# One product of the normed rows moved into each attention, in single steps between its units

## The reference

```python
gates = jax.nn.sigmoid(gate_logits.reshape(b, s, N_BRANCHES, d) + b_gate)
merged = gates[:, :, 0] * (o_a @ w_proj_a) + gates[:, :, 1] * (o_b @ w_proj_b)
x = x + (merged @ w_out)
```

## Time and profile before

| | |
|---|---|
| runs | 3157.65 us median of 3 (3156.02 to 3158.03) |
| profiled execution | span of the core 3155.9 us; the page gives no other time of it |
| TensorE busy | 2956.2 us, 94% |
| VectorE, ScalarE, GpSimd busy | 39%, 24%, 4% |
| mean granted clock of TensorE | 0.971 |

### The profile page before, as it was taken

One profiled execution on the slowest core, in us unless ns is written; L12 is line 12 of the kernel. 1 busy time (PEld: TensorE's weight loads), 2 busy tenths in 40 slices (PEclk: granted clock), 3 DMA queues, 4 the chain that ended last, 5 costly groups with the idle time before them and its releaser, 6 DMA issues.

```text
span 3155.9 us, 43167 instructions
## 1 busy us (share of the span) xinstructions
PE 2956.2 (94%) x15320; PEld 2056.7 (65%) x15321; DVE 1215.3 (39%) x2572; ACT 751.5 (24%) x1483; POOL 116.9 (4%) x132
## 2 busy tenths in 40 slices
PE   8989899998999999899899879898999999999999
PEld 7874667655585556386357668586776596776774
DVE  6770773242212221211212156535333355444432
ACT  3221751111212121211211023514111225232111
POOL 0000100000000000000000000011000000110000
PEclk9999999988999999999999989899999999999999
DMA  4222012257999999999999452021321220112221
GB/s 171 81 67 79 3 41 80 74 204 298 395 364 365 419 413 390 416 379 382 408 415 391 149 201 95 1 87 49 108 84 54 100 95 27 61 61 87 81 80 67
DMA packets 137804, 577.60 MB, mean 183 GB/s; under 512 B 15981, under 2 KB 21485, under 8 KB 87504
## 3 DMA queue, kind: packets, MB, share of 16 engines
q1 hardware_dynamic: 128176, 558.87, 46.6%
q0 software_dynamic: 9504, 17.07, 1.4%
HBM read 572.47 MB, written 20.97 MB: 188 GB/s over the span
## 4 chain that ended last, share of the span: by engine, by line
PE 85%; DVE 5%; DMA 5%; ACT 2%; issue 2%; DVEq 1%; SPq 0%; POOLq 0%; ACTq 0%
PE banks L395 31%; PE banks L1521 13%; PE banks L1497 9%; PE banks L332 8%; PE banks L1027 7%; PE banks L1471 6%; DMA arena<-in_w_experts 5%; PE banks L800 3%; PE banks L823 2%; PE banks L811 2%; PE banks L271 1%; DVE arena L873 1%; DVE arena L885 1%; PE banks L1451 1%; PE banks L1926 1%
## 5 line engine op out<-in xcount | busy, mean ns | idle before, releaser
L395 PE MATMUL banks<-arena 128*128 128x256 f32 (+2 forms) x4704 | 1015.3, 377 | 21.6 <-ACT arena L432 7.4
L395 PEld LDWEIGHTS banks<-arena 128*128 128x128 f32 x4704 | 883.8, 192 | 142.0 <-issue 21.5
L1521 PEld LDWEIGHTS banks<-arena 128*128 128x128 f32 x3584 | 403.8, 193 | 14.5 <-issue 14.5
L1521 PE MATMUL banks<-arena 128*128 128x128 f32 x3584 | 405.5, 277 | 4.7 <-issue 4.7
L1497 PE MATMUL banks<-arena 128*64 128x512 f32 (+1 forms) x1024 | 322.6, 593 | 0.0
L1471 PE MATMUL banks<-arena 128*64 128x512 f32 x1152 | 268.3, 616 | 24.9 <-DMA arena<-in_w_experts 22.3
L1599 DVE TENSOR_TENSOR arena<-banks,arena 128x512 f32<-128x512 f32 x64 | 44.3, 692 | 614.1 <-PE banks L1521 351.9
L432 ACT ACTIVATE arena<-banks 128x512 f32<-128x512 f32 (+2 forms) x168 | 98.7, 588 | 690.9 <-PE banks L395 690.9
L448 DVE TENSOR_TENSOR arena<-banks,arena 128x512 f32<-128x512 f32 (+2 forms) x126 | 85.7, 680 | 436.2 <-PE banks L395 434.7
L332 PE MATMUL banks<-arena 128*128 128x512 f32 x576 | 250.0, 593 | 0.0
L1497 PEld LDWEIGHTS banks<-arena 128*64 128x64 f32 (+1 forms) x1024 | 123.5, 159 | 176.1 <-issue 176.0
(11 more groups left out here) (210 smaller groups left out, 2041.0 us busy)
## 6 DMA issues: line engine op xcount, KB each, us to landing
arena<-in_w_experts SPq DMA_DIRECT2D x384, 1024.0 KB, 19.3
arena<-in_w_in SPq DMA_DIRECT2D x84, 1024.0 KB, 5.0
arena<-in_w_out SPq DMA_DIRECT2D x12, 1024.0 KB, 5.0
arena<-in_w_branch SPq DMA_DIRECT2D x24, 512.0 KB, 4.7
arena<-expert_rows SPq DMA_DIRECT2D x4, 2048.0 KB, 14.4
arena<-in_w_in SPq DMA_DIRECT2D x4, 832.0 KB, 4.6
arena<-in_gate_b SPq DMA_DIRECT2D x2, 1536.0 KB, 6.5
arena<-in_x SPq DMA_DIRECT2D x4, 512.0 KB, 5.3
```

What stands on the lines that cost most here:

```text
L395: last = PE.matmul(PS[:, bank, t * width:(t + 1) * width], one[:, t * P:(t + 1) * P], other, start=(first and t == 0 and kk == 0), stop=(t ...
L1521: last = PE.matmul(PS[:, q, f * P:(f + 1) * P], gate_up(q, k)[:, f * P:(f + 1) * P], xT[:, k], start=(f == 0 and k == 0), stop=(f == 3 and ...
```

## The change

In each attention 32 plain calls (4 row tiles by 8 steps of the contraction, 512 columns each) are issued by TensorE between the parts of its units. They make one product in bank 7; VectorE takes each finished tile out. The values of all pairs use bank 6.

- dilated and grouped: the logits of gate 0, first 512 columns, tiles 0, 2, 1 in units 4 to 15 of dilated and tile 3 in units 0 to 7 of grouped. In a layer's chunk attention the same, four units a tile.
- latent attention: `z` of the chunk branch, transposed, in units 2 to 15. Its weights are loaded behind the attention's fence into the place of raised queries and another free one.
- The merges begin with `branch` of branch 0; their first `Quarters` product is that of branch 1, and its weights are the ones issued ahead.
- The chunk heads have three products in place of four; sigmoid and multiplication of `z` run beside the first. They also load the gate's weights and bias, into places of their own.

The diff, cut:

```diff
@@ attention
+            def steps_of(u):
+                for t, (first, last) in enumerate(fill["units"] if fill else ()):
+                    if first <= u <= last:
+                        n, at = last - first + 1, u - first
+                        return list(range(8 * t + at * 8 // n, 8 * t + (at + 1) * 8 // n))
+                return []
+            def value_bank(p):
+                return 6 if fill else 6 + p % 2
+                def filling(steps):
+                    for n in steps:
+                        t, kk = n // 8, n % 8
+                        if n == 0:
+                            fill["ready"](pe, c)
+                        if kk == 0:
+                            pe.wait_ge(SEM[fill["out_sem"]], up(fill["out_count"](c) + t))
+                        last = PE.matmul(PS[:, 7], fill["still"](fill["tiles"][t], kk), fill["moving"](fill["tiles"][t], kk),
+                                         start=(kk == 0), stop=(kk == 7))
+                        if kk == 7:
+                            last.then_inc(SEM["fill_mm"], 1)
                 def values(u):
                     if i == 0:
-                        pe.wait_ge(SEM["o_done"], up(c.of("pairs") + p - 1))
+                        pe.wait_ge(SEM["o_done"], up(c.of("pairs") + p - (0 if fill else 1)))
                     if u + 2 < units:
                         scores(u + 2)
+                    steps = steps_of(u)
+                    filling(steps[:len(steps) // 2])
                     turn(u)
+                    filling(steps[len(steps) // 2:])
                     if u:
                         values(u - 1)
+                def filled(u):
+                    for n in steps_of(u):
+                        if n % 8 == 7:
+                            if n == 7:
+                                fill["ready_out"](dve, c)
+                            dve.wait_ge(SEM["fill_mm"], up(c.of("filled") + n // 8 + 1))
+                            fill["out"](fill["tiles"][n // 8], PS[:, 7]).then_inc(SEM[fill["out_sem"]], 1)
                 for u in range(units):
+                    if u:
+                        filled(u - 1)
                     if u + 2 < units:
                         top(u + 2)
                     if u + 1 < units:
                         norm(u + 1)
-                    if u % TT == 1 and u > TT:
+                    if u % TT == (0 if fill else 1) and u >= TT:
                         finish(u // TT - 1)
@@ attention_first
+            def next_gates(sp, c):
+                sp.wait_ge(SEM["fill_mm"], up(c.of("filled") + 1))
+                merge_1.lead(sp, c)
...
@@ merge_stage
             def lead(sp, c0):
-                dense_sp(sp, c0, 0, gate_weights(c0, 0, 0))
+                dense_sp(sp, c0, 0, gate_weights(c0, 0, 1))
...
-                        if n + b:
-                            dense_sp(sp, c, b, gate_weights(c0, n, b), quartered=b, done=-n * nbr)
+                        if n or b > 1:
+                            dense_sp(sp, c, b, gate_weights(c0, n, b), quartered=of_gates(n, b), done=-n * nbr)
                         sp.wait_ge(SEM["mm"], up(4 * (c.of("M") + b)))
...
-                        Q(c).pe(pe, c, 2 * b, b, hooks=hooks)
-                        branch(pe, c, b)
+                        if n or b:
+                            Q(c).pe(pe, c, b + of_gates(n, b), of_gates(n, b), hooks=hooks)
+                        branch(pe, c, n, b)
@@ latent_stages
+            def z_sp(sp, c):
+                sp_after(sp, c)
+                src = w2(c).rearrange("(k p) n -> p k n", p=P)[:, :, bass.ds(4000, 512)]
+                sp.dma_start(v2(QM, 6, 512), src[:, 0:6]).then_inc(SEM["fill_w"], 16)
+                sp.dma_start(v2(QST + 512, 2, 512), src[:, 6:8]).then_inc(SEM["fill_w"], 16)
+            z_fill = {"tiles": (0, 1, 2, 3), "units": ((2, 5), (6, 9), (10, 12), (13, 15)), ...
+                      "out": lambda t, ps: V.tensor_copy(v(YC + 512 * t, 512), ps)}
@@ chunk_stages
-            lead, sp0, pe_, act0, dve0 = fast_hT(0, [(c0s + 1536, 512), (c0s, 512), (c0s + 512, 512), (c0s + 1024, 512)],
-                                                        across=(0, 1, 2))
+            lead, sp0, pe_, act0, dve0 = fast_hT(0, [(c0s, 512), (c0s + 512, 512), (c0s + 1024, 512)], across=(0, 1))
...
+            gate_fill = {"tiles": (0, 1, 2, 3), "units": ((0, 3), (4, 7), (8, 11), (12, 15)), ...
+                         "out": lambda t, ps: V.tensor_tensor(v(early_gate(t), 512), ps, v(GATE_B, 512), ALU.add)}
```

More of the change, by code:

```diff
@@ L778, in attention @@
             first_group = [sum(groups_of[x % TT] for x in range(u)) for u in range(units + 1)]
-            KC = {"u": units, "g": first_group[units], "pairs": 4, "biased": 4 if a.get("sp") else 0}
+            fill = a.get("fill")
+            KC = {"u": units, "g": first_group[units], "pairs": 4, "biased": 4 if a.get("biased") else 0}
+            if fill:
+                KC["filled"] = len(fill["tiles"])
+                KC |= fill["counts"]
+            def steps_of(u):
[6 more added lines that the diff above has]
+                return 6 if fill else 6 + p % 2
             def prob(u, s):
@@ L1047, in sig, with part @@
                             act.wait_ge(SEM["sig_in"], up(c.of("sig") + 4 * b + tt + 1))
-                            g = v(GS + 512 * tt, 512)
+                            g = v(GS + 512 * tt if n or b else early(tt), 512)
                             AC.activation(g, g, ACT.Sigmoid).then_inc(SEM["sig_out"], 1)
+                        def part(i):
+                            Q(c).act(act, c, b + of_gates(n, b), of_gates(n, b), i)
+                        if not n + b:
+                            for tt in range(TT):
+                                sig(tt)
+                            continue
                         def back(tt):
@@ L1981, in finish, with z_weights @@
                 return V.tensor_tensor(o, ps, o, ALU.mult)
-            return latents, raised, turned, attention({"turn": (PTS, PTS + 1024), "scale": MLA_SCALE, "W": W_, "finish": finish,
+            def z_weights(kk):
+                return v(QM + 512 * kk, 512) if kk < 6 else v(QST + 512 * (kk - 5), 512)
+            def z_sp(sp, c):
+                sp_after(sp, c)
+                src = w2(c).rearrange("(k p) n -> p k n", p=P)[:, :, bass.ds(4000, 512)]
+                sp.dma_start(v2(QM, 6, 512), src[:, 0:6]).then_inc(SEM["fill_w"], 16)
+                sp.dma_start(v2(QST + 512, 2, 512), src[:, 6:8]).then_inc(SEM["fill_w"], 16)
+            z_fill = {"tiles": (0, 1, 2, 3), "units": ((2, 5), (6, 9), (10, 12), (13, 15)), "counts": {"fw": 2, "z_out": 4},
+                      "ready": lambda pe, c: pe.wait_ge(SEM["fill_w"], 16 * c.of("fw") + 32),
+                      "still": lambda t, kk: z_weights(kk)[:, t * P:(t + 1) * P], "moving": lambda t, kk: hT[:, kk],
+                      "out_sem": "z_out", "out_count": lambda c: c.of("z_out"), "ready_out": lambda dve, c: None,
+                      "out": lambda t, ps: V.tensor_copy(v(YC + 512 * t, 512), ps)}
+            return latents, raised, turned, attention({"fill": z_fill, "sp": z_sp, "turn": (PTS, PTS + 1024), "scale": MLA_SCALE, "W": W_, "finish": finish,
                 "scores": lambda p, s, i: [(v(MQT + s * 512 + p * 1024 + i * P, P, 96),
@@ L2056, in finish, with chunk_sp @@
                 return V.tensor_tensor(o, ps, o, ALU.mult)
-            return heads, attention({"turn": (LB + 6144, LB + 7168), "scale": ATT_SCALE, "W": W_, "finish": finish, "pool": biases, "sp": rows_of,
+            def chunk_sp(sp, c):
+                merge_2.lead(sp, c)
+                rows_of(sp, c)
+            gate_fill = {"tiles": (0, 1, 2, 3), "units": ((0, 3), (4, 7), (8, 11), (12, 15)), "counts": {"fw": 2},
+                         "ready": lambda pe, c: pe.wait_ge(SEM["fill_w"], 16 * c.of("fw") + 32),
+                         "still": lambda t, kk: hT[:, kk, t * P:(t + 1) * P], "moving": lambda t, kk: v(GATE_W + 512 * kk, 512),
+                         "out_sem": "sig_in", "out_count": lambda c: c.of("sig"), "ready_out": lambda dve, c: None,
+                         "out": lambda t, ps: V.tensor_tensor(v(early_gate(t), 512), ps, v(GATE_B, 512), ALU.add)}
+            return heads, attention({"fill": gate_fill, "biased": True, "turn": (LB + 13162, LB + 14186), "scale": ATT_SCALE, "W": W_, "finish": finish, "pool": biases, "sp": chunk_sp,
                 "scores": lambda p, s, i: [(v(CQK + p * 512 + i * P, P, E, E * s),
@@ L2121, in build @@
         heads_1 = project_first()
-        dilated, grouped = attention_first()
         merge_1, turn_last_1, mT = merge_stage(
@@ L2158, in _ @@
             heads_1.sp(sp, c)
-            merge_1.lead(sp, c)
+            dense_sp(sp, c, 0, lambda h: rows(w_in, 8, h, 5376, 512))
             dilated.sp(sp, c)
```

114 lines of the change are left out of this document (70 added, 44 removed).

## The result

The changed kernel takes 3161.11 us (median of 20 runs, 3156.51 to 3168.27); the kernel before, on the same chip, takes 3156.32 (20 runs, 3149.74 to 3161.78). The ratio is 1.0016, 95% interval 1.0009 to 1.0022: 5.0 us slower, between 2.8 and 6.9. That lies inside the 0.2% that the prediction called no change for most of its interval. It forecast 3161.5, or 3.9 more.

A forecast was written before the change was run, and what follows sets the result against it. TensorE was taken as the bound, holding 85% of the chain of waits. 137.4 - 121.7 - 28.1 - 15.0 + 24.4 + 6.9 = +3.9 us; 3161.5 us predicted, from a median of 3157.65, range over the cases 3149 to 3177.

The forecast's parts named there:

- Removed, 121.7: Merges and head projections: five products by quarters go, 24.47 + 2 x 24.41 + 2 x 24.2 = 121.7 us.
- Added, 137.4: Attentions: five plain products of 32 steps, 0.86 us a step, add 5 x 64 x 0.429 = 137.4 us.
- Hidden waits: Attentions: steps cover 28.1 us of TensorE's waits (bounds 20 and 32): grouped 0.8, latents 13.0, chunks 14.3.
- The dilated 0.31: Dilated unit: TensorE's 0.31 us wait inside the transposes gets no step, so it stays.
- four copies out of the bank ... fit: Latent attentions: VectorE, busy 12.05 of 16.5 us, has room for four copies of some 0.7 us each.
- Clock won back, 15.0: Latent and chunk attentions: without pauses the clock recovers, 6.8 in latents, 7.4 and 0.8 in chunks, 15.0 us (bounds 0, 20.7).
- Rival A: Attentions: the lower clock is not won back, price 15.0 us; +18.9 on the time before, 3176.5; chance 0.22.
- The new wait, 24.4: Merges: branch 0's product waits for weights issued behind fence and bias broadcast, 7.8 + 2 x 8.3 = 24.4 us.
- Rival B: Merges: weights pass or run beside the bias broadcast, waits 4.5 each; 11 less, low clock 2 less: -9, 3148.5; chance 0.12.
- The low clock after it, 6.9: Merges: after TensorE's pause of 8 us the clock is low, losing 2.3 at each, 6.9 us (bounds 0 and 10).
- Rival C: Attentions: 18 handovers of the single bank for values stall 0.7 us each; +12.6 on the forecast, 3174; chance 0.07.
- Rival D: Attentions: VectorE and ScalarE freed, clock wholly back also in starts (20.7), grouped hides 2.2; -3.2, 3154.5; chance 0.12.

The follow-up runs named there:

- experiment 7: Changed kernel with the dilated attention's step ahead of the transposes put inside them, before the third group: 3152.55 us, ratio 0.9991 to the kernel before.
- experiment 11: Changed kernel with the layers' first branch weights loaded during the chunk attention and the dilated step inside the transposes: 3133.59 us, ratio 0.9927 to the kernel before.
- experiment 10: Changed kernel with the layers' first branch weights loaded during the chunk attention into places of their own: 3139.11 us, ratio 0.9943 to the kernel before.
- experiment 1: Kernel before with only the z projection filled into the two latent attentions: 3145.03 us against 3154.33, ratio 0.9964.
- Experiment 6: Changed kernel with the eight z steps of a tile all in one unit of the latent attentions: 3178.13 us, ratio 1.0065 to the kernel before.
- experiment 2: Kernel before with only the first block's gate 0 filled into dilated and grouped, its merge starting with the branch product: 3172.93 us, ratio 1.0064.
- experiment 4: Changed kernel with the first branch's weights issued ahead of the gate bias broadcast in each merge: 3151.50 us, ratio 0.9990 to the kernel before.
- experiment 5: Changed kernel with eight unused calls ahead of each merge's first branch product: 3154.70 us, ratio 0.9997 to the kernel before.
- experiment 9: Changed kernel with the first block as in the kernel before, the layers' z and gate fills kept: 3147.56 us against 3155.82, ratio 0.9974.

## Why the prediction was right, step by step

**Removed, 121.7.** Right: the quarter products' line fell by 560 records, the head stages by 24.2 each.

**Added, 137.4.** Nearly: 0.88 in the dilated units and 0.86 in the grouped ones where 0.858 was taken. The charge that I named and left out was 0.05 for a step standing alone; dilated shows about half of it, grouped none.

**Hidden waits.** The dilated 0.31 stayed as said, and experiments 7 and 11 show that it was on the path. Grouped absorbed 1.6 us, but hid nothing: its waits for normalised probabilities are 3.5 us before and 3.7 after. What it won is clock, on which the prediction counted nothing there. Behind the same first wait the transposes ran at the lower clock before (granted 0.50) and at the full one after (1.00):

```profile
PE banks L811 <- DVE arena L885: 3.5, 4, 1.7
...
PE banks L827 <- DVE arena L916: 3.7, 3, 1.7
...
406.98 1.97 PE L811 MATMUL banks<-arena 128*128 128x128 f32 x8 [1.67 <-DVE arena L885]
...
431.34 1.10 PE L827 MATMUL banks<-arena 128*128 128x128 f32 x8 [1.67 <-DVE arena L916]
```

That the clock did not fall here in this profile is luck: in experiments 7, 10 and 11 the filled grouped attention has 3.4 us at the lower clock in its first units and takes 62.7 to 62.9 in place of 61.3.

In the chunk attentions 16.5 became 1.8, so 14.7 where 14.3 was said, and the wait that stays at the start is 0.9 (predicted 1.1):

```profile
2167.45 0.44 PE L827 MATMUL banks<-arena 128*128 128x128 f32 x2 [0.92 <-DVE arena L916]
```

In the latents 13.0 was too much. At unit 0 of the first latent TensorE waits 1.33 us, before the steps begin (unit 2). In the kernel before there was no such wait, because the first scores ran at the lower clock (granted 0.50, 5.46 us where they now take 3.24). And twice in each a step waits 0.33 us for the copy of the tile before out of bank 7, a wait that the prediction had no term for ("four copies out of the bank ... fit"). The two on TensorE's timeline:

```profile
2021.59 0.44 PE L827 MATMUL banks<-arena 128*128 128x128 f32 x2 [1.33 <-DVE arena L916]
...
2043.31 1.13 PE L838 MATMUL banks<-arena 128*128 128x512 f32 x2 [0.33 <-DVE arena L2073]
```

13.0 less 1.7, 0.3 and twice 0.6 leaves 9.8 in this pair. Over all profiles TensorE stands 7.0 us on the mean in an unfilled latent and 1.6 in a filled one, 10.9 in two. That is the mis-sized term: the latents with their heads gained 11.1 by the table and 11.3 by experiment 1, where 13.2 was forecast. In the chunk attentions the same count gives 9.3 and 1.5, so 15.7 in two.

**Clock won back, 15.0.** The lower level is a granted 0.50 (2022 to 2027 us of the kernel before). The 15.0 were worked out from rows 6: 8.71 us at 0.61 lose 3.4, taken once in each latent attention, and the four stretches of the chunk attentions lose 2.6, 2.7, 3.9 and 4.7, 6.5 of it at the starts. The expectation was right: all four attentions run at 1.00 past their starts. In the chunk attentions 25.0 of the 55.0 us were absorbed, 15.7 of it waits, so about 9.3 is clock (8.2 forecast). In the latents 17.7 were absorbed, 10.9 of it waits, so about 6.8 (6.8 forecast). The granted clock says the same: an unfilled chunk attention spends 6.8 to 17.1 us at the lower level, a filled one none in twenty; a latent 3.4 to 16.5 unfilled (11.2 on the mean) and 0 to 10.2 filled (4.3), all of it in the first 12 us. The exact 6.8 is luck. The prediction counted one stretch in each latent, where the first latent before has three, and did not say that the one at the start would mostly stay. Experiment 6 ties the clock to the waits: spacing the same steps so that the waits return brings the low clock back. Rival A had this failing; it is out. The tie is not strict, though. In experiment 2 the first latent attention (from 2013.21) is that of before and waits, and its clock does not fall before 2060; it took 52.31, the least of the six. Its waits up to 2056 and the stretch:

```profile
PE banks L827 <- DVE arena L916: 5.4, 4, 1.4
...
2000.00:2056.00 56.00, 47.17 (x316) 30.45 (x314) 34.89 (x142) 33.08 (x90) 0.00 (x0) 1.00 0.00 1
```

**The new wait, 24.4.** Right: with the fence's own 1.25 and 1.83 taken off, 6.8 + 2 x 8.4 = 23.6. Just under half of it (11.0) comes from the order of the two issues, which experiment 4 turns round. It is Rival B's mechanism, as something that one can do and not as something that the change did: B's waits (4.5 each) would have needed the weights to pass the broadcast, and they did not. With the order turned, the waits are 4.2 each beside the fence's own. B's price was right there, but not its 2 us less of low clock.

**The low clock after it, 6.9.** Right in sum: 3.0 + 2.5 + 1.4 = 6.8 by experiment 5. In the first merge the granted clock is 0.50 from 495 to 500 us, behind the 8.06 us of wait for the weights, and the product takes 16.90 us; with the eight calls in that wait it is 1.00 throughout, and the same product takes 13.93.

**Rival C, the single bank of values.** Out: TensorE waits for no `finish` in any attention after.

**Rival D, and what cancels.** Half of D came true: the chunk attentions have their clock back from the start on, and grouped has it too. Clock and hidden waits together make 44.3 us in the table's terms, where 28.1 + 15.0 = 43.1 was forecast: some 26 of waits where 28.1 were said, and some 18 of clock where 15.0 were. That the sum is so near is partly luck. So is the nearness of 3161.11 to 3161.5: the sum was added to a median of 3157.65, and the kernel before then measured 3156.32.

**What the profile pair shows and the change did not do.** The dilated attention starts with two waits for a row maximum, 3.03 and 2.56 before, 3.97 and 3.76 after, 2.1 us more, and its third scores come 3.2 us later. The same longer waits stand in experiment 1, whose first block is that of before, while experiment 9 has 3.02 and 2.58. It goes either way in kernels with the same first block, so it isn't the change. A VectorE instruction shows where it is made; VectorE and GpSimd after:

```profile
315.75 1.80 DVE L907 TENSOR_SCALAR arena<-arena 128x2 f32<-128x2 f32 x1
322.61 1.63 DVE L907 TENSOR_SCALAR arena<-arena 128x2 f32<-128x2 f32 x1
...
315.50 2.02 POOL L959 COPY arena<-arena 128x512 f32<-128x512 f32 x2
322.19 2.02 POOL L959 COPY arena<-arena 128x512 f32<-128x512 f32 x2
```

Two columns take 1.80 and 1.63 us and end when GpSimd's pair of copies ends (317.52, 324.21). In the kernel before the same instruction took 0.86 and ended about with the first copy of such a pair (315.89 to 316.75; the pair runs from 315.64 for 2.06).

**What stays open.** The first block's part alone measured 20 us, and 13.2 as the difference of two kernels. The parts alone sum to 14 and the whole is 5.0. Stages account for 11.9 and 3.2. No stage of a profile holds the 7 or 8 us by which experiment 2 is slower than that; its profile is of its fastest run (3166.4). It is one comparison with five runs of that kernel, and the two intervals just meet, so it may be scatter; the cause is not known. The 0.27 us of experiment 7 is measured and not explained.

## What to carry to other kernels

Filling the waits of an attention with single steps of another product absorbs the waits and the low clock that mostly comes with them (9 and 12.5 us an attention here), if the steps stand in each unit; an attention without waits, as the dilated one, absorbs nothing, and giving up the cheaper algorithm cost 15.7. A product that is moved also takes its cover away from the transfers issued beneath it: here they cost 30 us with the clock, of 44 that the filling won, and loading two of the three a stage earlier turned +5 into -18. Before moving work, list what was issued beneath it, and move those issues too.

## What the runs showed of the hardware

- Two DMAs on one queue, a broadcast of 1.5 MB and then 2 x 0.5 MB: the weights land 8.1 us after issue; issued the other way round, 4.4 us.
- The same branch product of 32 records takes 16.90, 16.48 or 15.41 us behind pauses of 8.06, 10.29 and 10.26, 15.58 behind 6.06, and 13.97 behind 1.83. The longer pause doesn't cost more: over all kernels the product takes 15.4 to 16.9 behind pauses of 5.5 to 10.3 us. One pause, that of the first merge (7.9 to 8.2 us in six kernels), was followed by 15.40, 15.42, 15.50, 15.88, 16.90 and 16.93.
- A VectorE instruction on two columns took 1.80 us while GpSimd copied. It ended when the second of two copies did (317.55 and 317.52); in the kernel before it took 0.86. Why is not shown: no run here took GpSimd's copies away.
- A filled chunk attention is steady (64.74 to 64.76 us in twenty), one with waits is not (48.3 to 51.6 in six). A filled latent attention still scatters at its start (72.4 to 74.8 in eighteen).
